# Two transformer blocks in one program: meta queries in column groups, small vector loads spread between ring loads

## What is computed

```
def neighbourhood_attention(q, k, v, rpb, meta_bias):
    qm, km, vm = q[:, :N_META], k[:, :N_META], v[:, :N_META]
    s_mm = jnp.einsum('bqhd,bkhd->bhqk', qm, km) * scale + meta_bias[None, :, None, :]
    p_mm = jax.nn.softmax(s_mm, axis=-1)
    meta_out = jnp.einsum('bhqk,bkhd->bqhd', p_mm, vm)
    ...
def mla_attention(...):
    def attend(qb):
        s = jnp.einsum('bqhd,bkhd->bhqk', qb, k) * scale
        p = jax.nn.softmax(s, axis=-1)
        return jnp.einsum('bhqk,bkhd->bqhd', p, v)
    out_meta = attend(q[:, :N_META])
    ...
    return h[:, N_META:]
```

## Time and profile before

| | us |
|---|---|
| time before, median of 3 runs | 2693.52 (2691.1 to 2695.06) |
| profiled execution, its own time | 2680.49 |
| profiled execution, span from first to last instruction | 2678.9 |
| PE busy in that span | 2565.4 (96%) |
| DVE busy | 1439.2 (54%) |
| ACT busy | 1029.3 (38%) |
| mean granted TensorE clock | 0.967 of full speed |

### The profile page before, as it was taken

How to read it: one execution, slowest core, us unless ns; L and a number is a source line. 1 busy time by engine, 2 the same in 40 slices (tenths; PEclk the granted TensorE clock), 3 DMA queues, 4 the chain that set the end, 5 groups by cost and what they waited for, 6 DMA issues and landing times.

```text
span 2678.9 us, 47978 instructions
## 1 busy us (share of the span) xinstructions
PE 2565.4 (96%) x20066; PEld 2413.6 (90%) x20066; DVE 1439.2 (54%) x1932; ACT 1029.3 (38%) x1313; POOL 288.9 (11%) x371
## 2 busy tenths in 40 slices
PE   6899989989999999999989998999999999999998
PEld 4898857989999999999989996867899999999998
DVE  3577756965764444434354544734655555554343
ACT  3433244334334434333333335423444444443333
POOL 5000122410000000011113002103000000000000
PEclk8999989979999999999979999989999999999999
DMA  9777867947785555555544441312455555555553
GB/s 328 266 250 269 301 222 266 335 144 240 251 286 189 185 179 184 175 174 187 172 131 146 125 150 49 112 63 90 145 175 187 176 184 172 188 180 181 183 178 110
DMA packets 263873, 504.17 MB, mean 188 GB/s; under 512 B 17168, under 2 KB 26299, under 8 KB 263483
## 3 DMA queue, kind: packets, MB, share of 16 engines
q1 hardware_dynamic: 257915, 494.98, 55.3%
q10 hardware_dynamic: 5840, 7.52, 0.9%
HBM read 498.05 MB, written 2.10 MB: 187 GB/s over the span
## 4 chain that ended last, share of the span: by engine, by line
PE 78%; DVE 9%; ACT 5%; DMA 4%; issue 3%; SPq 1%; POOL 0%; DVEq 0%; ACTq 0%
PE bank L2005 23%; PE bank L2007 22%; PE bank L2006 22%; ACT w_hi L872 3%; DMA raw<-in_w_in 3%; DVE w_lo L1353 3%; PE bank L2093 2%; PE bank L2122 1%; PE bank L2040 1%; DVE tmp L1486 1%; SPq L606 1%; DVE ada_acc L1381 1%; PE bank L2314 1%; DVE acc_beside L1522 1%; PE bank L2147 1%
## 5 line engine op out<-in xcount | busy, mean ns | idle before, releaser
L1353 DVE TENSOR_TENSOR w_lo<-raw,w_hi 128x2048 fp32r<-128x2048 f32 (+3 forms) x386 | 862.9, 2236 | 989.8 <-ACT w_hi L872 989.4
L2005 PE MATMUL bank<-x_hi,w_hi 128*128 128x256 f32 (+2 forms) x4608 | 1322.4, 287 | 40.1 <-DVE w_lo L1353 27.1
L2006 PE MATMUL bank<-x_lo,w_hi 128*128 128x256 f32 (+2 forms) x4608 | 1310.3, 284 | 0.0
L2007 PE MATMUL bank<-x_hi,w_lo 128*128 128x256 f32 (+2 forms) x4608 | 1309.4, 284 | 0.0
L872 ACT ACTIVATE w_hi<-raw 128x2048 fp32r<-128x2048 f32 (+3 forms) x386 | 718.6, 1862 | 1082.4 <-PE bank L2007 924.9
L2005 PEld LDWEIGHTS bank<-x_hi,w_hi 128*128 128x128 f32 x4608 | 875.7, 190 | 77.4 <-DVE w_lo L1353 37.4
L2007 PEld LDWEIGHTS bank<-x_hi,w_lo 128*128 128x128 f32 x4608 | 877.8, 190 | 0.0
L2006 PEld LDWEIGHTS bank<-x_lo,w_hi 128*128 128x128 f32 x4608 | 873.8, 190 | 1.2 <-issue 1.2
L2005 PE MATMUL bank<-hid_hi,w_hi 128*128 128x256 f32 x1408 | 399.2, 284 | 2.1 <-DVE x_res L1900 1.0
L2006 PE MATMUL bank<-hid_lo,w_hi 128*128 128x256 f32 x1408 | 398.4, 283 | 0.0
L2007 PE MATMUL bank<-hid_hi,w_lo 128*128 128x256 f32 x1408 | 398.4, 283 | 0.0
(11 more groups left out here) (309 smaller groups left out, 1512.7 us busy)
## 6 DMA issues: line engine op xcount, KB each, us to landing
raw<-in_w_ada SPq DMA_DIRECT2D x88, 1024.0 KB, 6.0
raw<-in_w_gate SPq DMA_DIRECT2D x88, 1024.0 KB, 5.2
raw<-in_w_up SPq DMA_DIRECT2D x88, 1024.0 KB, 5.2
raw<-in_w_in SPq DMA_DIRECT2D x68, 1024.0 KB, 6.1
raw<-in_w_down SPq DMA_DIRECT2D x64, 1024.0 KB, 5.0
raw<-in_w_down SPq DMA_DIRECT2D x32, 768.0 KB, 4.3
raw<-in_w_o SPq DMA_DIRECT2D x16, 1024.0 KB, 6.5
raw<-in_w_out SPq DMA_DIRECT2D x16, 1024.0 KB, 5.0
```

Source lines behind the costliest of these rows:

```text
L1353: dve.tensor_tensor(w_lo[ps][:, 0:width], raw[slot][:, 0:width], w_hi[ps][:, 0:width], ALU.subtract).then_inc(raw_free[slot], 1)
L2005: pe.matmul(out, wh[:, k, c], hi(k0 + k), start=a0, stop=False)
L2006: pe.matmul(out, wh[:, k, c], lo(k0 + k), start=False, stop=False)
L2007: ins = pe.matmul(out, wl_[:, k, c], hi(k0 + k), start=False, stop=z)
```

## The change

**Small loads.** SP issues them one by one, each between the load of a `w_ada` unit and that of the `w_in` unit of the same block: those of `PACKS[1]` in part 0 (blocks 4 to 9), those of `PACKS[2]` in part 1 (one name a block), `PACKS[3]` in part 1's last block, `causal` at part 2's block 0, `mbias` at part 2's block 2. `mbias8` is gone. The transposes of `packs` move from u = 20 to u = 23, `lambdas` from u = 21 to u = 25.

```
+            def small_loads(part, n):
+                if part == 0 and n >= 4:
+                    load_pack(sp, 1, vec_in, range(n - 4, n - 3))
+                elif part == 1 and n < 10:
+                    load_pack(sp, 2, vec_in, range(n, n + 1))
+                elif part == 1:
+                    load_pack(sp, 3, vec_in)
+                elif part == 2 and n == 0:
+                    sp.dma_start(causal[:, :], a["causal"]).then_inc(causal_in, 16)
+                elif part == 2 and n == 2:
+                    sp.dma_start(mbias[:, :, 1:META + 1], bias.unsqueeze(0).broadcast_to([P, 8, META])).then_inc(
+                        mb_in, 16)
             for part in range(4):
                 for n, j in enumerate(ORDER_IN1):
-                    if part == 1 and n == 2:
-                        for pack in range(1, 4):
-                            load_pack(sp, pack, vec_in)
...
                     if n < 8:
                         ada_of(part, n)
+                    small_loads(part, n)
```

```
+            def meta_scores(q, n):
+                pe.wait_ge(n_app, norm_end("mla_k" if q else "na_k1", "use"))
+                for r in range(2):
+                    out = bank[7 - r][:, 0:n] if q else bank[4][:, n * r:n * r + n]
+                    for j in range(4):
+                        h = 4 * r + j
+                        query, key = (qn(h), kn(h)) if q else (proj2[:, T2_Q + h, :], proj2[:, T2_K + h, N2 - n:N2])
+                        ins = pe.matmul(out[32 * j:32 * j + 32, :], query[:, S:S + 1].broadcast_to([P, 32]), key,
+                                        start=True, stop=not q)
+                    for j in range(4 if q else 0):
+                        h = 4 * r + j
+                        ins = pe.matmul(out[32 * j:32 * j + 32, :], qr(h)[:, S:S + 1].broadcast_to([64, 32]), kr(h),
+                                        start=False, stop=True)
...
+            def meta_out(q):
+                pe.wait_ge(m_copied, q + 1)
+                first = 0 if q else 2
+                for r in range(2):
+                    for k in range(first, 3):
+                        for j in range(4):
+                            c, h = slice(32 * j, 32 * j + 32), 4 * r + j
+                            stay = turned_m[:, r, c] if k == 2 else turned_k[:, r, k, c]
+                            ins = pe.matmul(bank[7][c, 2 * P + P * r:3 * P + P * r], stay,
+                                            vtok2[0:META if k == 2 else P, k, h, :], start=k == first, stop=k == 2)
...
+            def meta_back(q):
+                pe.wait_ge(m_rows, q + 1)
+                for r in range(2):
+                    ins = pe.transpose(bank[6][:, P * r:P * r + P], rows_m[:, r, :], ident)
```

More of the change, by code:

```diff
@@ L378, in program @@
             sem("head_" + s) for s in ("scored", "masked", "exp", "normed", "turned", "copied", "out", "taken", "low"))
-        m_query, m_scored, m_masked, m_exp, m_normed, m_turned, m_copied, m_out, m_taken = (
-            sem("meta_" + s) for s in ("query", "scored", "masked", "exp", "normed", "turned", "copied", "out",
+        m_scored, m_masked, m_exp, m_normed, m_turned, m_copied, m_out, m_rows, m_back, m_taken = (
+            sem("meta_" + s) for s in ("scored", "masked", "exp", "inverse", "turned", "copied", "out", "rows", "back",
                                        "taken"))
@@ L563, in unit, with load_pack @@
             return src, nk, nc_
-        def load_pack(eng, j, done):
-            for name, row, rows in PACKS[j]:
+        def load_pack(eng, j, done, some=slice(None)):
+            for name, row, rows in PACKS[j][slice(some.start, some.stop)]:
                 r0 = row - P * j
@@ L1689, in heads @@
                     if meta >= 0 and g == g0:
-                        meta_normalise(meta, keys)
+                        meta_inverse(meta)
                     normalise(g)
@@ L1783, in meta_mask @@
-                dve.tensor_scalar(mstat[:, 0:1], mstat[:, 2:3], -1.0, None, ALU.mult).then_inc(m_masked, 1)
-            def meta_normalise(q, n):
+                    both = bank[4][:, 0:2 * META].rearrange("p (r k) -> p r k", r=2)
+                    chain(*[dve.scalar_tensor_tensor(mrow_na[32 * j:32 * j + 32, :, :], both[32 * j:32 * j + 32], NA_SCALE,
+                                                     mbias[32 * j:32 * j + 32, j:8:4, 0:META], ALU.mult, ALU.add)
+                            for j in range(4)])
@@ L2370, in heads @@
                         scores(g + 2)
+                    q = g0 // 8 - 2
                     if g >= 16 and g == g0 + 1:
[L2372 removed]
+                        meta_out(q)
+                        out(g0)
+                        meta_back(q)
+                        pe.wait_ge(m_taken, 2 * q + 2)
                     turn(g)
                     if g >= 16 and g == g0:
[L2375 to L2376 removed]
+                        meta_turn(q, META if g0 == 16 else N2)
+                    elif g > g0 and not (g >= 16 and g == g0 + 1):
                         out(g - 1)
@@ L2559, in _ @@
             pe.wait_ge(bank_freed, 4 + 4 * FREED_NA)
-            heads(24, 32, lambda: meta_scores(1, N2, bank[7]))
+            heads(24, 32, lambda: meta_scores(1, N2))
             pe.wait_ge(h_taken, 32)
```

129 lines of the change are left out of this document (61 added, 68 removed).

## The result

| | before | changed |
|---|---|---|
| median of 5 runs shown with the change | 2691.10 us | 2672.43 us |
| ratio (95% interval) | | 0.9927 (0.9910 to 0.9944) |
| the profiled execution, its span | 2680.49, 2678.9 us | 2672.79, 2671.0 us |
| mean granted clock of TensorE | 0.967 | 0.970 |

The change is faster by 18.7 us (0.7%) in the median, and the interval of the ratio leaves out 1; 22.4 had been summed up against one execution. The 2691.10 of before is the median of five runs; the 2693.52 that the prediction starts from was that of three. Where those 10.6 us were is a part of the answer.

A forecast was written before the change was run, and what follows sets the result against it. PE, busy 96% of the span, was taken as the bound. The terms -9.8 + 0.5 + 2.5 - 15.9 + 0.7 - 1.0 + 0.6 gave -22.4 us, from a median of 2693.52 to 2671.1, range 2661 to 2682.

The forecast's parts named there:

- Item 1: First projection: with small loads no longer in a row, part 1 becomes as long as part 2, -9.8 us.
- item 3: First projection, part 2: mbias right before a w_in load delays that load, +2.5 us, bounds 0 and +5.
- Item 2: First projection: issuing 21 small loads one at a time delays hungry ring loads, +0.5 us, bounds 0 and 2.
- the first projection gives nothing: First projection: mbias costs 5 us, other small loads 2, part 1 keeps a 3 us stall; 2678 us, chance 0.14.
- Items 4 to 6: MLA's meta query: scores, transposes, products and waits take 7.8 us in place of 23.7, -15.9 us.
- The clock, +0.7: MLA's meta query: 0.7 us added for the chance that the gaps bring the clock down.
- The rule on draining at a change of tiling mode: MLA's column groups: a tiling mode change drains the engine; four at 0.30 us would make the sum 1.2 us higher.
- Item 7: NA: products of 0.7 us and a wait of about 1.5 replace 1.9 and 0.9; -1.0 us, bounds -2.5 and +1.
- Item 8: Eight one-column products for the scale, 16 records where PE is the bound, +0.6 us, not below 0.5.
- No overlap: MLA's meta query: column groups do not overlap, scores 7.5 us, products 5.3; 2680 us, chance 0.07.
- The clock falls after the new gap: MLA, after the 2.1 us gap: work at the lower clock costs 1.7 to 3.5 us; 2674 us, chance 0.10.
- Each small load interrupts the queue: First projection: the ring restarts only after each of 21 small loads, 1.5 us each; slower, 2700 us, chance 0.04.

The follow-up runs named there:

- e1_loads: Kernel before with only the new, spread places of the small loads, meta query left old; 2693.94 us, 1.0003 of before.
- e3_mbias_part1: Changed kernel with the mbias load moved to part 1, at the block where the row of small loads stood before; 2670.58 us, 0.9916 of before.
- e3_row_late: Changed kernel with the 20 other small loads in a row in part 1, mbias just before the first MLP's down projection; 2666.40 us, 0.9895 of before.
- e2_serial: Changed kernel with the meta query's products reordered head by head, neighbours mostly in the same column group; 2688.76 us, 0.9983 of before.

## Why the prediction was right, and where it wasn't

The time was predicted at 2671.1 and is 2672.4 to 2674.6; the gain was predicted at 22.4 and is 18.7. That the time came out this near is luck in good part. It is two errors of opposite sign, which the halves show: 6.8 from the small loads, measured 0; 15.6 from the meta query, measured 22.5. And 2.4 of the 3.7 us that the gain is short of are hidden by the start, the median of three runs, which lay 2.4 above that of five.

- **Item 1, -9.8 for the small loads.** This step failed in its size and in what it put the price on. Part 1 became 3 to 7 us shorter (81.6 and 80.3 before; 74.6 and 77.0 in after, 74.2 in e1_loads), not 9.8: it is 74 to 77 without `mbias`, so part 2's 71.7 was not its undisturbed length. And the gain is not that of issuing the loads one by one: with them one by one and `mbias` in its old place part 1 is 80.2 (e3_mbias_part1), with them in a row and `mbias` away it is 77.0 (e3_row_late). What item 1 gained is `mbias` leaving part 1, and item 3 pays it back.
- **Item 2, +0.5.** Not contradicted: with the 20 single loads part 1 is 74 to 77, no longer than the 77.0 with them in a row.
- **Item 3, +2.5 for `mbias`.** This step failed: 5.5 to 7. I took the cover of 1 MB of `w_ada` for half a cover. The trace shows that load done at 195 with the queue nearly dead for the small rows right after it (0.43, 0.08 and 0.41 from 194 to 200), and the next block landing late by it; its price is that and the lower clock that the stall brings (0.50 at 204). My own reading of the earlier trace rows gave the bound, +5, the price at the old place; the middle had no row of its own. The rule of the Trainium skill, "DMA: Bandwidth & Descriptors", section on where the 2 us go, that descriptor generation is small, would have made this term 0. The page says it of the path by which GpSimd issues transfers, and these are issued by SP. The term measured 5.5 to 7; as 128 rows the same bytes left the DMA share at 1.04 in the window where 1024 rows left it at 0.08. Whether it is the making of the descriptors or the moving of the small rows that takes this time, no run here shows.
- **The rival "the first projection gives nothing"** is what happened, with `mbias` at its full price, the first of its three terms; the other two, 2 for the hungry ring and 3 left in part 1, are seen only as part 1 at 74 to 77 in place of 72. Its time of 2678 was wrong, because the rest of the sum was too small.
- **Items 4 to 6, from the meta scores to group 28: 15.9 us less.** Measured 16.1 in the first profile. Term by term: scores 2.37 (2.0), turning 0.66 (0.7), products 1.85 (2.0), the gap ahead of the transposes 0.68 (1.0), standing at `m_taken` 1.78 (2.1). e2_serial shows that the overlap of column groups was the right reason, and that it hangs on the order: neighbours of one shape in different groups.
- **The clock, +0.7.** This step failed, on the side of before. The sum is made against the profiled execution, and to carry the difference to the median over supposed that all of these 13 us lay outside the change. The other two executions of the old query lie 14.7 and 16.8 us above the first in their spans, and 3.2 and 7.9 of that in the stretch that the change removes, behind its last landmark: the low clock of the old products lasts 17, 24 or 34 us. Another 5.0 lie between 330 and 445 us, where the supposition held. All 9 profiles with the new products in their given order have no fall there. The gain is therefore 16.2, 19.5 or 24.2 to group 30. The +0.7 for a fall of the clock in the new stretch was not needed.
- **The rule on draining at a change of tiling mode** (the Trainium skill, "TensorEngine Tiling (Array Packing)", key properties) would have cost 1.2 by my reading of it. The trace agrees in kind and not in size: no idle time stands at the changes, but each set of four takes 0.59, with a change of rows (128 or 64) at its end, where a product of one unchanging shape took 0.47. That is 0.1 a change and some 0.5 in all, which is the 2.37 in place of 2.0. Whether it is a drain the trace does not say.
- **Item 7, NA -1.0:** measured -0.9 in the first profiles and -0.5 in the second (17.74 and 17.24), by the way predicted, with a wait of 0.78 for DVE's division where I had left room for one.
- **Item 8, +0.6:** the 16 records lie within 0.3 us, and the next product begins 0.2 behind the first of them, so the term was twice to three times too large.
- **The other rivals.** No overlap: refuted by 2.37. The clock falls after the new gap: not in nine profiles, though e2_serial shows it falling there once the products ahead are slow. Each small load interrupts the queue: refuted, part 1 at 74 to 77.

## What to carry to other kernels

Before a gain is summed against one profiled execution, look at where the removed stretch ends: if the clock is low in it, the cost runs on behind it, by an amount that differs from execution to execution. An execution well below the median may be one in which it was short; a second profile shows how much of the difference lies there and how much in places that the change leaves alone. A load of many small rows is priced by the queue that stands behind it; here it cost nothing that was seen where the queue was slack, ahead of the down projection, and 5 us or more between two large loads of a hungry stage, although 1 MB was in flight ahead of it. Products in column groups pay only in sets, one product of the same shape for each group; written head by head, the same products cost more than the form that they replace.

## What the runs showed of the hardware

In the stretch of one-column products PE is busy for 5.00 of 5.00 us and its weight loads for 4.89, and the granted clock of that stretch is 0.50; with four column groups and 128 columns moving it stayed at 1.00. The low clock set in 1.2 to 2.3 us after such products began (four profiles) and lasted 17, 24, 31 or 34 us, long after they had ended: the heads behind them, which run at 1.00 in the nine profiles with the new products, paid for it. Before the fall PE is as busy: in e1_loads the products begin at 1790.40 and the clock is at 1.00 until about 1792.5 with PE at work without a gap.

Products in sets of four groups take 0.59 us for eight records, 272 columns moving; head by head they take 0.57 for two.

One thing stays unexplained. From ACT's 257th split to its 385th, the second MLP for the most part, it is 724.1 us in all three profiles with the old meta query and 723.1 to 723.3 in the eleven others, though the change touches nothing there.
